# The output projection of a hybrid decoder step, rewritten from two-tile loops into straight-line code with the engines one tile apart

## The reference, cut to what matters

```python
def rms_norm(x, gain):
    xf = x.astype(jnp.float32)
    y = xf * lax.rsqrt(jnp.mean(xf * xf, axis=-1, keepdims=True) + EPS)
    return (y * gain.astype(jnp.float32)).astype(x.dtype)
```

## Time and profile before

| | |
|---|---|
| time, median of 3 runs | 4760.25 us (4759.86 to 4765.94) |
| profiled execution: own time | 4747.01 us |
| profiled execution: span | 4745.8 us |
| PE busy over the span | 4002.0 us, 84% |
| mean granted clock of TensorE | 0.875 |
| matmuls of `mix` (544 passes) | 239.1 us busy |
| transposes of `mix` (136) | 17.7 us busy |
| first matmul of `mix` starts at | 2924.62 us |
| last low of `mix` ends at | 3185.06 us |

### The profile page before, as it was taken

One profiled execution on the slowest core, in us unless ns is written; L12 is line 12 of the kernel. 1 busy time (PEld: TensorE's weight loads), 2 busy tenths in 40 slices (PEclk: granted clock), 3 DMA queues, 4 the chain that ended last, 5 costly groups with the idle time before them and its releaser, 6 DMA issues. The chain is left out here.

```text
span 4745.8 us, 51217 instructions
## 1 busy us (share of the span) xinstructions
PE 4002.0 (84%) x19290; PEld 3200.2 (67%) x19290; DVE 2129.2 (45%) x4175; ACT 1488.0 (31%) x2357; POOL 689.5 (15%) x547
## 2 busy tenths in 40 slices
PE   8697786787739898888877636989999999979999
PEld 5454444454438777777767624449999999968877
DVE  2367888988933443433331471223434444430200
ACT  2004555665613444444421101112222222221211
POOL 0100000000012222222200002111111111114433
PEclk9798898898856888988875566999999999989999
DMA  2223221120131111111014003321111111145433
GB/s 92 86 89 69 65 50 52 45 56 27 47 109 33 44 29 37 35 35 32 12 30 160 0 3 113 106 82 36 44 45 54 36 54 54 36 128 173 129 107 115
DMA packets 285868, 302.54 MB, mean 64 GB/s; under 512 B 33652, under 2 KB 230420, under 8 KB 279383
## 3 DMA queue, kind: packets, MB, share of 16 engines
q1 hardware_dynamic: 270170, 256.80, 18.6%
q10 hardware_dynamic: 13408, 22.44, 1.4%
q0 software_dynamic: 2112, 20.97, 1.2%
HBM read 206.35 MB, written 94.10 MB: 63 GB/s over the span
## 5 line engine op out<-in xcount | busy, mean ns | idle before, releaser
L519 PE MATMUL chan_p_g<-ht,chan_w 128*128 128x412 f32 (+1 forms) x1920 | 730.6, 526 | 36.1 <-ACT chan_flat L560 20.1
L1632 PE MATMUL up_p_g<-ht_high,up_wh 128*128 128x412 f32 (+1 forms) x1760 | 617.3, 351 | 0.1
L1632 PE MATMUL up_p_g<-ht_low,up_wh 128*128 128x412 f32 (+1 forms) x1760 | 615.4, 350 | 0.0
L1632 PE MATMUL up_p_g<-ht_high,up_wl 128*128 128x412 f32 (+1 forms) x1760 | 615.2, 350 | 0.0
L519 PEld LDWEIGHTS chan_p_g<-ht,chan_w 128*128 128x128 f32 x1920 | 373.4, 197 | 298.6 <-issue 242.9
L2032 ACT ACTIVATE chan_signed<-chan_sc,chan_trial 128x512 bf16<-128x512 f32 (+6 forms) x224 | 305.0, 1362 | 146.5 <-DVE chan_trial L2087 132.2
L1650 ACT ACTIVATE up_pre<-up_p_g 128x412 f32<-128x412 f32 (+1 forms) x220 | 113.3, 515 | 748.8 <-PE up_p_g L1632 748.8
L1632 PEld LDWEIGHTS up_p_g<-ht_high,up_wh 128*128 128x128 f32 x1760 | 331.6, 188 | 1.7 <-issue 0.5
L1632 PEld LDWEIGHTS up_p_g<-ht_low,up_wh 128*128 128x128 f32 x1760 | 331.3, 188 | 1.2
L1632 PEld LDWEIGHTS up_p_g<-ht_high,up_wl 128*128 128x128 f32 x1760 | 331.2, 188 | 0.5
L2073 DVE TENSOR_SCALAR_CACHE_REDUCE chan_tie<-chan_sc,chan_trial 128x384 bf16<-128x384 f32 (+6 forms) x224 | 316.1, 1411 | 7.5
(11 more groups left out here) (518 smaller groups left out, 6784.1 us busy)
## 6 DMA issues: line engine op xcount, KB each, us to landing
down_a<-scratch_act SPq DMA_DIRECT2D x88, 512.0 KB, 3.7
scratch_act<-up_acc SPq DMA_DIRECT2D x22, 1028.0 KB, 5.2
up_w<-in_w_up SPq DMA_DIRECT2D x44, 512.0 KB, 6.4
chan_iq<-scratch_iq SPq DMA_DIRECT2D x28, 512.0 KB, 7.2
scratch_qkv<-chan_acc SPq DMA_DIRECT2D x12, 1028.0 KB, 3.9
chan_w<-in_w_in SPq DMA_DIRECT2D x24, 512.0 KB, 4.2
mid_raw<-scratch_qkv SPq DMA_DIRECT2D x16, 768.0 KB, 5.4
proj_x<-in_x_prompt SPq DMA_DIRECT2D x16, 512.0 KB, 3.6
```

The lines of the kernel that those rows point to most:

```text
L519: last = pe.matmul(p_g[at % BANKS][:, 0:cols.stop - cols.start], w[n % 2][:, k, :], K.ht[:, k, cols], start=(k == 0), stop=(k == KD - 1))
L1632: last = pe.matmul(p_g[u][:, 0:cols.stop - cols.start], wp[s][:, k, :], hp[:, k, cols], start=(k == 0 and m == 0), stop=(k == KD - 1 and m ...
```

## The change

`mix` is written as straight-line code for all 17 tiles, without loops on the device and without `credit`. The steps of a tile are the same instructions on the same engines with the same shapes. What differs:

- The order on each engine. In step j PE does mult(j) and then turn(j-3) (before: turn(j-1)). DVE does add(j-1), the reciprocal and xn of tile j-2, h(j-4), and mean(j-1). ACT does Square(j-1), high(j-5), sqrt(j-1). Steps whose tile is outside 0 to 16 are left out.
- `x` has three buffers instead of two.
- `stat` has a column for each tile.
- ACT issues the weights as eight transfers of 512 KB, each with its own semaphore. In mult(0) PE waits for each piece ahead of the two matmuls that use it.
- SP issues `m` of tiles 0 and 1 first, then `gain`, then `x` of tiles 0 and 1. `gain` has its own semaphore, for which DVE alone waits.
- SP's order per tile is now load of `m`, store, load of `x`.

The block has 28 semaphores instead of 27. The lines of the old code stand in full above, so the diff shows of them only a few; "..." marks what is left out.

```diff
@@ -1397,140 +1397,141 @@
 def mix(nc, K, x_prompt, x_sample, w_out, norm_ffn):
...
+    XRING = 3
     with phase(nc, "mix") as (c, stack):
...
-        m, x, xn = two("m", [P, KD, P]), two("x", [P, D]), two("xn", [P, D])
+        m, xn = two("m", [P, KD, P]), two("xn", [P, D])
+        x = [c.sb(f"x{b}", [P, D]) for b in range(XRING)]
...
-        stat = two("stat", [P, 4])
+        stat = c.sb("stat", [P, 4, TILES])
...
-        s_w = c.sem("w")
...
+        s_w = c.sems("w", KD)
+        s_gain, s_mm, s_x2, s_sum, s_mean, s_root, s_inv, s_norm, s_turn, s_ht, s_high, s_low = (
+            c.sem(n) for n in "gain mm x2 sum mean root inv norm turn ht high low".split())
+        s_m, s_x, s_st = c.sems("m"), c.sems("xin", XRING), c.sems("st", XRING)
         block = open_block(nc, stack, c)
...
+        rows_of = lambda t: slice(t * P, t * P + P) if t < NT else slice(SEQ, TOK)
+        count_of = lambda t: P if t < NT else DEC
+        inside = lambda t: 0 <= t < TILES
+        END = TILES + 5
 
         @block.sync
         def _(sp):
-            credit(sp, c)
-            sp.dma_start(gain[:, :], norm_ffn.rearrange("(k p) -> p k", p=P), allow_slow_non_contiguous=True)\
...
+            def load(t):
+                n = count_of(t)
+                if t >= 2:
+                    sp.wait_ge(s_mm, t - 1)
+                sp.dma_start(m[t % 2][:, :, 0:n], K.d_mix[:, :, rows_of(t)].rearrange("k p n -> p k n")).then_inc(s_m[t % 2], 16)
+
+            def residual(t):
+                n = count_of(t)
+                if t >= XRING:
+                    sp.wait_ge(s_norm, t - XRING + 1)
+                    sp.wait_ge(s_st[t % XRING], t // XRING * 16)
+                sp.dma_start(x[t % XRING][0:n, :], x_prompt[rows_of(t), :] if t < NT else x_sample).then_inc(s_x[t % XRING], 16)
+
+            def store(t):
+                n = count_of(t)
+                sp.wait_ge(s_x2, t + 1)
+                sp.dma_start(K.d_x2[rows_of(t), :], x[t % XRING][0:n, :]).then_inc(s_st[t % XRING], 16)
+            load(0)
+            load(1)
+            sp.dma_start(gain[:, :], norm_ffn.rearrange("(k p) -> p k", p=P), allow_slow_non_contiguous=True).then_inc(s_gain, 16)
+            residual(0)
+            residual(1)
+            for j in range(2, TILES + 2):
+                if inside(j):
+                    load(j)
+                store(j - 2)
+                if inside(j):
+                    residual(j)
+            for b in range(XRING):
+                sp.wait_ge(s_st[b], len(range(b, TILES, XRING)) * 16)
 
         @block.tensor
         def _(pe):
...
-            pe.wait_ge(s_w, 4 + 32)
...
+            for j in range(END):
+                if inside(j):
+                    pe.wait_ge(s_m[j % 2], j // 2 * 16 + 16)
+                    if j >= 2:
+                        pe.wait_ge(s_x2, j - 1)
+                    for k in range(KD):
+                        if j == 0:
+                            pe.wait_ge(s_w[k], 16)
+                        for half in range(2):
+                            last = pe.matmul(p_y[j % 2][:, half, :], m[j % 2][:, k, :], w[:, k, half * 512:(half + 1) * 512],
+                                             start=(k == 0), stop=(k == KD - 1))
+                    last.then_inc(s_mm, 1)
+                t = j - 3
+                if inside(t):
+                    pe.wait_ge(s_norm, t + 1)
+                    if t >= 2:
+                        pe.wait_ge(s_ht, t - 1)
+                    for k in range(KD):
+                        last = pe.transpose(p_t[t % 2][:, k, :], xn[t % 2][:, k * P:(k + 1) * P], K.ident[:, :])
+                    last.then_inc(s_turn, 1)
 
         @block.scalar
         def _(act):
-            act.dma_start(w[:, :, :], w_out.rearrange("(k p) n -> p k n", p=P)).then_inc(s_w, 16)
...
+            for k in range(KD):
+                act.dma_start(w[:, k, :], w_out[k * P:(k + 1) * P, :]).then_inc(s_w[k], 16)
+            for j in range(1, END + 1):
+                t = j - 1
+                if inside(t):
+                    act.wait_ge(s_x2, t + 1)
+                    if t:
+                        act.wait_ge(s_sum, t)
+                    act.activation(junk[:, :], x[t % XRING][:, :], ACT.Square, accum_out=stat[:, 0, t:t + 1]).then_inc(s_sum, 1)
+                t = j - 5
+                if inside(t):
+                    n = count_of(t)
+                    act.wait_ge(s_ht, t + 1)
+                    act.activation(K.ht[:, :, t * P:t * P + n], h[:, :, 0:n], ACT.Copy).then_inc(s_high, 1)
+                t = j - 1
+                if inside(t):
+                    act.wait_ge(s_mean, t + 1)
+                    act.activation(stat[:, 2, t:t + 1], stat[:, 1, t:t + 1], ACT.Sqrt).then_inc(s_root, 1)
 
...
+            for t in range(TILES):
+                n = count_of(t)
+                cols = slice(t * P, t * P + n)
+                pool.wait_ge(s_high, t + 1)
                 pool.tensor_tensor(K.hl[:, :, cols], h[:, :, 0:n], K.ht[:, :, cols].bitcast(F32), ALU.subtract).then_inc(s_low, 1)
...
         @block.vector
         def _(dve):
-            dve.wait_ge(s_w, 4 + 32)
...
+            dve.wait_ge(s_gain, 16)
+            for j in range(1, END):
+                t = j - 1
+                if inside(t):
+                    dve.wait_ge(s_x[t % XRING], t // XRING * 16 + 16)
+                    dve.wait_ge(s_mm, t + 1)
+                    dve.tensor_tensor(x[t % XRING][:, :], p_y[t % 2][:, :, :].rearrange("p a n -> p (a n)"), x[t % XRING][:, :], ALU.add)\
+                       .then_inc(s_x2, 1)
+                t = j - 2
+                if inside(t):
+                    dve.wait_ge(s_root, t + 1)
+                    dve.reciprocal(stat[:, 3, t:t + 1], stat[:, 2, t:t + 1]).then_inc(s_inv, 1)
+                    dve.wait_ge(s_inv, t + 1)
+                    if t >= 2:
+                        dve.wait_ge(s_turn, t - 1)
+                    dve.tensor_scalar(xn[t % 2][:, :], x[t % XRING][:, :], stat[:, 3, t:t + 1], None, ALU.mult).then_inc(s_norm, 1)
+                t = j - 4
+                if inside(t):
+                    dve.wait_ge(s_turn, t + 1)
+                    if t:
+                        dve.wait_ge(s_low, t)
+                    dve.tensor_tensor(h[:, :, :], p_t[t % 2][:, :, :], gain[:, :].unsqueeze(2).broadcast_to([P, KD, P]), ALU.mult)\
+                       .then_inc(s_ht, 1)
+                t = j - 1
+                if inside(t):
+                    dve.wait_ge(s_sum, t + 1)
+                    dve.tensor_scalar(stat[:, 1, t:t + 1], stat[:, 0, t:t + 1], 1.0 / D, EPS, ALU.mult, ALU.add).then_inc(s_mean, 1)
```

More of the change, by code:

```diff
@@ L1408, in mix @@
         p_t = [c.ps(f"t{b}", [P, KD, P]) for b in range(2)]
-        s_w = c.sem("w")
-        s_m, s_x, s_mm, s_x2, s_sum, s_mean, s_root, s_inv, s_norm, s_turn, s_ht, s_st = (
-            c.sems(n) for n in "m x mm x2 sum mean root inv norm turn ht st".split())
-        s_high, s_low = c.sem("high"), c.sem("low")
+        s_w = c.sems("w", KD)
+        s_gain, s_mm, s_x2, s_sum, s_mean, s_root, s_inv, s_norm, s_turn, s_ht, s_high, s_low = (
+            c.sem(n) for n in "gain mm x2 sum mean root inv norm turn ht high low".split())
@@ L1413, in mix @@
+        s_m, s_x, s_st = c.sems("m"), c.sems("xin", XRING), c.sems("st", XRING)
         block = open_block(nc, stack, c)
-        LAST = NT // 2
+        rows_of = lambda t: slice(t * P, t * P + P) if t < NT else slice(SEQ, TOK)
+        count_of = lambda t: P if t < NT else DEC
+        inside = lambda t: 0 <= t < TILES
+        END = TILES + 5
         @block.sync
         def _(sp):
-            credit(sp, c)
-            sp.dma_start(gain[:, :], norm_ffn.rearrange("(k p) -> p k", p=P), allow_slow_non_contiguous=True)\
[L1420 to L1445, removed]
@@ L1471, in _ @@
-            turn(LAST, 0)
+            for j in range(END):
[18 more added lines that the diff above has]
+                    last.then_inc(s_turn, 1)
@@ L1503, in _ @@
-            low(LAST, 0, DEC)
         @block.vector
         def _(dve):
-            dve.wait_ge(s_w, 4 + 32)
[L1509 to L1533, removed]
+            dve.wait_ge(s_gain, 16)
```

6 lines of the change are left out of this document (removed).

## The result

The changed kernel takes 4772.21 us (median of 15 runs, 4764.79 to 4776.04), the kernel before, run beside it, 4760.25 us (15 runs, 4755.05 to 4767.32). The ratio is 1.0020, with a 95% interval of 1.0012 to 1.0028. The ratio compares the means, 4771.06 and 4761.54 us: slower by 9.5 us, between 5.7 and 13.3. The medians lie 12.0 us apart. The forecast was 10.3 us slower.

The account below looks back on a forecast made before the run. PE was taken to bound the kernel, busy 84% of the span. Start -0.7, transposes -1.7 and tail +12.7 us sum to +10.3: 4757.3 us against the profiled execution, 4770.5 as a median; range 4762 to 4776.

Parts of the forecast that it names:

- The middle: Between first and last mult: PE never waits at 14.61 us per tile, so reordering and the third `x` buffer gain 0.
- Two groups of transposes: On PE before mult(16) ends: 13 groups instead of 15, at 0.87 us each, 1.7 us less.
- The start: Before PE's first matmul: `m`, first on SP's queue, lands sooner but shares engines with the weights; 0.7 us less.
- The bound of 10 us sooner: At the start: best case, `m` and early weight pieces come through first and PE starts 10 us sooner.
- The tail: From add(16) to the block's end: DVE owes four h instead of two, serial through one `h`; 12.7 us more.
- the round trip: In the tail: from one h through high and low to the next h, 5.03 us.
- `m` did not come through early: Rival at the start: `m` lands early, PE starts up to 10 us sooner, 4761 us; chance 0.09.
- The loops: Rival on PE: each loop turn stalls at its branch, so straight-line code is faster, 4750 us; chance 0.05.
- Slow pieces: Rival at the start: pauses between the eight weight transfers; 3 us each would cost some 8 us, 4779; chance 0.04.
- the bound of 0.2%: Whole kernel: a change below 0.2%, 9.5 us, counts as about indistinguishable from none; the forecast lay just above.

Follow-up runs that it names:

- second pair: Kernel before and changed kernel, each profiled a second time without an edit; `mix` stages 282.0 and 292.1 us.
- e1_lag2: Changed kernel with turn, h and high one tile nearer to mult; ratio to the kernel before 1.0012.
- e4_one_w: Changed kernel with the weights as one 4 MB transfer again; `mix` stage 291.7 us against 291.6, ratio not timed.
- e5_m_on_act: Changed kernel with `m` of tile 0 issued by ACT ahead of the weight pieces on the same queue; ratio to the kernel before 1.0001.
- e2_old_order: Changed kernel, still straight-line with the new start, but with the old order on PE, DVE and ACT; ratio to the kernel before 0.9990.
- e3_gain_first: Changed kernel with `gain` issued first on SP's queue again; `mix` stage 291.5 us against 291.6, ratio not timed.
- e6_two_h: Changed kernel with a second buffer for `h`; ratio to the kernel before 1.0000.

## Why the prediction was right

The forecast was +10.3 us, with the terms -0.7, -1.7 and +12.7. The first pair of profiles gives -0.6, -1.7 and +11.8, in sum +9.5, the second pair 0.0, -1.7 and +11.8, in sum +10.1. The timed difference is 9.5 us (5.7 to 13.3).

- *The middle is worth nothing.* Right. The period is 14.61 us in every kernel of the table with one group of transposes per mult, whatever stands around it.
- *Two groups of transposes leave the path.* Right, 1.7 us, and e1_lag2, which puts one back, pays 0.9.
- *The start.* Right in its main reason: PE was released by `m`, which shares the engines with the weights to their end and lands some tenths behind them (in e4_one_w the weights at 2937.6, `m` at 2938.1). The size, 0.7, can't be told from these profiles. The two pairs give 0.6 and 0.0, and the six kernels with the changed start reach add(0) between 33.0 and 35.3 us, against 35.4 before; that 0.6 came out is luck as much as working. The working itself, 1024 rows that end with 1024 rows because they take turns, is only half of it. SP's queue is served from 3 to 4 us after its first issue, and its rows then go one for one, but not 1024 of them: in e4_one_w some 700 of `m` had gone by 2936, and the rest went in a rush as the weights ended. `gain`, which the prediction read as let through at the weights' pace, passed 545 of its 1024 elements by 2921 and the rest in the next 1.3 us. The rows are in the last section. The bound of 10 us sooner was within reach: e5_m_on_act reaches 9.3, but it needs one queue rather than the first place on another. The Trainium skill, "DMA: Bandwidth & Descriptors", section "Queues, rings and completion order", says that a DMA engine takes turns between queues, and that a turn is a packet of some 9 to 17 descriptors. The turns agree with these runs; turns of that length don't, taking a row for a descriptor: in windows of 0.2 and 0.3 us, in which a DMA engine moves one or two rows of the weights, the two queues passed 22 and 21 packets, and 31 and 31 (before).
- *The tail.* The mechanism was right in each link. low(12) starts 3.4 us after add(16) (3.64 in the working), h(13) at 5.9 (6.09), h(16) at 20.6 (21.43), and high(13) stands behind sqrt(16). The size was 0.9 too large. The term that was off is the round trip: 5.03 us, read from a tile inside the loop of before, where the straight-line code needs 4.85. From h(13) to h(16) it is 14.7 us rather than 15.3, and h(13) came 0.2 sooner; together the 0.9. e2_old_order, with the order of before and no loop, has 4.82, so the 0.2 go with the loop's form of high and low; why an instruction costs more there, no run shows.
- *The rivals.* `m` did not come through early. The loops hide no stall on PE: e2_old_order keeps 232.8 us between the adds, to the tenth. Slow pieces: e4_one_w, with one transfer, has the stage of after within 0.1 us.

The forecast stood close to the bound of 0.2%, and so does the result: the interval holds values on either side of it.

## What to carry to other kernels

Running the engines further apart helps only where some engine waits in the middle. Here none did, and each tile of distance was paid back at the end, at the price of one serial round trip through the single buffer `h`. Count what is still owed when the last piece of the bounding engine's work ends, and how fast that can drain; a second buffer, or finishing each tile inside the shadow of the next, takes it off.

A small transfer that gates the start belongs at the head of the same queue as the bulk that it would otherwise compete with. As long as it lands last, cutting the bulk into pieces gives nothing (e4_one_w); that the pieces pay once it is first is argued from e5_m_on_act and not run by itself.

## What the runs showed of the hardware beyond that

*While both are served, two queues share row by row, not by bytes.* Below, q10 is ACT's queue with the weights, 4 KB a packet, and q1 SP's; behind the colon stand packets, MB and the share of the 16 engines. First `before` from 2919.3 to 2919.5, where q1 carries `gain`, 4 bytes a packet; then e4_one_w from 2932 to 2934 and after from 2938 to 2940, where q1 carries `m` of tiles 0 and 1, 512 bytes a packet:

```profile
q10 hardware_dynamic: 22, 0.09, 112.7%
q1 hardware_dynamic: 21, 0.00, 6.1%
```

```profile
q10 hardware_dynamic: 171, 0.70, 86.5%
q1 hardware_dynamic: 173, 0.09, 15.1%
```

```profile
q10 hardware_dynamic: 192, 0.69, 87.6%
q1 hardware_dynamic: 193, 0.09, 16.4%
```

From the first pair a row of the weights takes some 0.16 us of its DMA engine. Turns of nine rows would last about 1.5 us on an engine, and a sum of whole turns in a window of 0.2 us would seldom come out level. The neighbouring windows from 2918.0, 2918.2 and 2918.4 have 19 and 20, 21 and 21, 20 and 19.

Two things go against a plain rule. SP's queue starts late: `m` was issued at 2927.66 after the change, and from 2928.5 to 2930 q10 has 146 packets and q1 none. And with the weights in pieces it first catches up, from 2930 to 2932:

```profile
q10 hardware_dynamic: 121, 0.43, 57.2%
q1 hardware_dynamic: 431, 0.22, 40.0%
```

By 2938 q1 had passed 1035 rows over all DMA engines, more than the 1024 of the first `m`, which still landed only at 2941.9, so probably some DMA engines were on rows of the second `m` while others owed rows of the first. Why it catches up, and which DMA engines lag, no run shows.

*How long the clock stays low at a start varies between profiles of the same instructions.* In the six kernels with the changed start mult(0) took 15.7 to 17.2 us, a spread of 1.5. The windows from the first matmul, after the change and in e6_two_h:

```profile
2941.90:2945.00 3.10, 3.10 (x4) 1.48 (x5) 0.00 (x0) 0.00 (x0) 0.00 (x0) 0.50 1.07 299
2945.00:2948.00 3.00, 3.00 (x5) 1.19 (x4) 0.00 (x0) 0.00 (x0) 0.00 (x0) 0.60 0.21 85
```

```profile
2946.70:2949.80 3.10, 3.10 (x4) 1.51 (x5) 0.00 (x0) 0.00 (x0) 0.00 (x0) 0.50 1.08 273
2949.80:2952.80 3.00, 3.00 (x8) 1.24 (x7) 0.00 (x0) 0.00 (x0) 0.00 (x0) 0.97 0.40 164
```

The clock stands ahead of the last two columns: 0.50 and 0.60 in one, 0.50 and 0.97 in the other, from 1.2 GHz to nearly all 2.4. A difference of a microsecond in one profile's start is no evidence, then, which is one reason why e3_gain_first stays open.

*DVE stood still while POOL worked, once.* In e6_two_h xn(16) took 2.59 us, where the 16 others took 0.75:

```profile
3197.27 2.59 DVE L1523 TENSOR_SCALAR mix_xn<-mix_x,mix_stat 128x1024 f32<-128x1024 f32 x1
```

It is the only xn there with a low beside it (POOL from 3196.96 on), and it ends some 0.6 us after the first of those lows would end (3196.96 + 2.34). The Trainium skill, "SBUF — State Buffer", section "SBUF: two separate sides", says that VectorE in some modes and GpSimd lock a shared pair of ports for a whole instruction, and that the other waits; the trace agrees, with 1.84 us. The three h of the same stretch, which read `p_t` and lie beside lows too, took 1.21 to 1.23 us, no longer than elsewhere. With one `h` no low of the tail or the middle has an instruction of DVE beside it.
